# Two VectorE steps change places in the third up-projection unit

## The chip, the cores and the metric

The kernel runs on one core of one Trainium2 chip. Its time is device microseconds of one execution. The kernel before has a median of 1523.43 us over 3 runs (1523.28 to 1523.55). Five engines work side by side and meet through semaphores: TensorE (PE in the profile, its weight loads PEld), VectorE (DVE), ScalarE (ACT), GpSimd (POOL) and SyncE (SP), which issues the DMAs.

## The reference, cut to what matters

One layer of a streaming encoder, in float32, for 1024 tokens of width 1024: a mixer sub-layer (gated linear recurrence beside a spatial gating unit), then a channel sub-layer, then a final norm. The change lies in the channel sub-layer:

```python
h = _modulated_norm(x, norm_ffn_g[l], shift2, scale2)
hid = _causal_dwconv(h @ w_up[l], ffn_conv_w[l], ffn_conv_b[l])   # w_up: 1024 x 6144, conv of width 3
act, val = jnp.split(hid, 2, axis=-1)
x = x + gate2[:, None, :] * ((jax.nn.gelu(act) * val) @ w_down[l])
```

## The kernel before

Everything is transposed: channels on partitions, tokens along the free axis. The up-projection is cut into 24 units `("U", u)`, u from 0 to 23; each makes 128 channels of `act` and the 128 channels of `val` that belong to them, for all 1024 tokens. The third unit, u = 2 (`PLAIN = 2` in the code), is the first that is computed by seven products instead of eight (Strassen-Winograd on a 2 x 2 partition of weights and tokens).

**Two pieces of every number.** A float32 operand is split into a high piece, a copy in a shorter format made by ScalarE (`hi`, L1313), and a low piece, the rest, made by VectorE (`lo`, L1901: `wop low = raw - wop high`). A product of TensorE (`product7`, L886) is 12 matmuls: four k-steps, and for each high x high, high x low, low x high. It waits for the low of its weights, `ready(n)`. The seven weight operands of a unit have the numbers n0 to n0 + 6; the text calls the lows of unit 2 low 1 to low 7 (`lo(n0)` to `lo(n0 + 6)`), and `lo(n0 + 7)`, `lo(n0 + 8)` the next unit's low 1 and 2. Four buffers `wop` hold the pieces and six buffers `raw` the weights themselves.

**The right sides.** Four quarters of the normed activations (`hq`) and four sums or differences of them (`v1q` to `v4q`) lie ready as two pieces each. The lows of the four differences are made once, by `t_low(0)` to `t_low(3)` (L2658, 128 x 2048). The last of them, for `v4q`, is made inside unit 2, whose seventh product is the first to need it.

**Joins.** Products accumulate in PSUM onto each other. ScalarE takes three snapshots of half-made sums (`snap`, L1328), and VectorE adds them where they belong (`join(pos, 0)` to `join(pos, 2)`, L1915; joins 1 to 3 in the text). The seventh product waits for join 2.

**Other steps of VectorE in a unit.** It finishes the unit before: two convolution taps on each of two tiles (`conv_tap`, L2588, reading PSUM) and the product of the gelu and the other half (`gate_mul`, L2600), which waits for the last tap and for the gelu of ScalarE. From every two units it makes parts for the down-projection: `part_sum` (L2625) and `part_low` (L2637), which SyncE stores (`hid_keep`).

**GpSimd** makes the four weight sums of the next unit, four passes of 128 x 512 from SBUF to SBUF (`weight_sums`, L727, L730, L734, L738; passes 1 to 4 in the text). Pass 1 writes into the buffer of the operand of low 6, so it waits for low 6; pass 2 follows pass 1; passes 3 and 4 wait for the next unit's lows 1 and 2.

Each engine runs its instructions in the order in which the program is written. For VectorE this is the loop `for w in range(7)` at L2712: the steps of one unit by slots w, with `lo(n0 + w + 3)` at the end of a slot. The lines that the change touches:

```python
if w >= 4 and not (soon and w < 6):        # L2713
    join(pos, w - 4)
...
if w == 2 and u == PLAIN:                  # L2728
    t_low(3)
...
if n0 + w + 3 < n_ops and (w or kind == "U" and u != PLAIN) and not (late and w == 4)\
        and not (soon and w == 4):
    lo(n0 + w + 3)                         # L2767
```

Of the kernel before, what the change touches and what calls it, by code (L numbers as in the profile page):

```python
# [17 lines left out]
def build(nc, a, out):  # L18
# [7 lines left out]


    _, S, D = a["x"].shape
    KT = D // P
    NB = S // P  # L30
# [42 lines left out]
    with ExitStack() as ctx:  # L73
# [243 lines left out]
        PLAIN = 2  # L317
# [452 lines left out]
        def _(pe):  # L770
# [20 lines left out]
            def param_columns(t):  # L791
                n = sum(n for _, n in ROWS[t])
                return nc.tensor.transpose(ps[0][:, min(t, 1), t * P:t * P + n], prow[0:n, t, :], ident[0:n, 0:n])
# [1092 lines left out]
        def _(dve):  # L1886
# [11 lines left out]
            def lo(n):  # L1898
                dve.wait_ge(f_hi, n + 1)
                kd = depth[n]  # L1900
                V.tensor_tensor(wop[n % 4][:, 1, 0:kd, :], raw[slot_of[n][0]][:, 0:kd, :], wop[n % 4][:, 0, 0:kd, :].bitcast(F32),  # L1901
                                ALU.subtract).then_inc(f_lo, 1)

            def join(pos, i):
                act_t, val_t = BANKS[pos % 2]
                n0, base = first_op[SEQ[pos]], 3 * block_unit[SEQ[pos]]
                u2 = snap_u2r if pos <= AT["ZV", 0] else snap_u2
                p1, p5 = (snap_o1, snap_o5) if SEQ[pos][0] == "O" else (snap_p1, snap_p5)
                out_b, in_b, kept, left, taken = (
                    (act_t[:, 1, :], act_t[:, 1, :], u2, n0 + 3, 3),  # L1910
                    (val_t[:, 1, :], val_t[:, 0, :], p5, n0 + 4, 2),
                    (act_t[:, 0, :], act_t[:, 0, :], p1, n0 + 5, 1))[i]
                dve.wait_ge(*used_at[left])
                dve.wait_ge(snapped, base + taken)
                V.tensor_tensor(out_b, in_b, kept[:, :], ALU.add).then_inc(joined, 1)  # L1915
# [291 lines left out]
            for pos in range(2, AT["B", 0]):  # L2207
                item = SEQ[pos]
                n0 = first_op[item]
# [113 lines left out]
            for pos in range(AT["B", 0], AT["B", 3]):  # L2323
                kind, i = SEQ[pos]
                n0 = first_op[kind, i]
# [162 lines left out]
            for i in range(3):  # L2488
                pos = AT["O", i]
                n0 = first_op["O", i]  # L2490
# [90 lines left out]
            def conv_tap(u, s, d, pos):  # L2581
                dst, src = hidw[hid_slot(u)][:, 1 - s, :], flat(BANKS[pos % 2][s])
                f, k = u + s * FT, FW - 1 - d
                if d == 1:
                    dve.wait_ge(tap0ab, 2 * u + s + 1)
                else:
                    dve.wait_ge(vch, conv_at[u, s])
                tap = V.scalar_tensor_tensor(dst[:, d:S], src[:, 0:S - d],  # L2588
                                             C("ffn_conv_w01" if k < 2 else "ffn_conv_w2", k % 2 * 2 * FT + f), dst[:, d:S],
                                             ALU.mult, ALU.add)  # L2590
                if d == 1:
                    conv_at[u, s] = step_number(tap)
                else:
                    tap.then_inc(taps_done, 1)

            def gate_mul(u):
                w = hidw[hid_slot(u)]
                dve.wait_ge(ga_ready, u + 1)
                dve.wait_ge(taps_done, 2 * u + 2)
                V.tensor_tensor(w[:, 1, :], w[:, 1, :], w[:, 0, :], ALU.mult).then_inc(g_ready, 1)  # L2600
# [47 lines left out]
            def middle_evict(m, pos):  # L2648
                dve.wait_ge(tile_done, m + 1)
                V.scalar_tensor_tensor(xT[:, m, :], flat(BANKS[pos % 2][m % 2]), mod[:, 5 * KT + m:5 * KT + m + 1],  # L2650
                                       xT[:, m, :], ALU.mult, ALU.add).then_inc(down_used, 1)

            def t_low(i):
                dst, src = ((v1q, v1w), (v2q, v2w), (v3q, v3w), (v4q, n21))[i]
                dve.wait_ge(sum_hi, IN_HI + O_PARTS + i + 1)
                if i == 1:
                    dve.wait_ge(t_made, O_SUMS + 4 * KH)
                V.tensor_tensor(dst[:, 1, :, :], src[:, :, :], dst[:, 0, :, :].bitcast(F32), ALU.subtract).then_inc(sum_lo, 1)  # L2658
# [29 lines left out]
            for pos in range(NF + PLAIN, len(SEQ) - 1):  # L2688
                kind, u = SEQ[pos]
                n0 = first_op[kind, u]  # L2690
                j = u // 2 - 1
                if kind == "M":
                    conv_tap(FT - 1, 0, 1, pos - 1)
                    conv_tap(FT - 1, 0, 2, pos - 1)
                    middle_evict(0, pos)
                    lo(n0 + 3)
                    conv_tap(FT - 1, 1, 1, pos - 1)
                    middle_evict(1, pos)
                    conv_tap(FT - 1, 1, 2, pos - 1)
                    middle_evict(2, pos)  # L2700
                    gate_mul(FT - 1)
                    middle_evict(3, pos)
                    lo(n0 + 4)
                    hid_low(FT - 1)
                    middle_evict(4, pos)
                    lo(n0 + 5)
                    for m in range(5, KT):
                        middle_evict(m, pos)
                    lo(n0 + 6)
                    continue  # L2710
                for w in range(7):
                    soon = kind == "U" and u == PLAIN + 2  # L2712
                    if w >= 4 and not (soon and w < 6):  # L2713
                        join(pos, w - 4)
                    if soon and w == 4:
                        join(pos, 0)
                        lo(n0 + w + 3)
                        join(pos, 1)
                    if w == 0:
                        if kind == "D" or u == PLAIN:  # L2720
                            lo(n0 + 3)
                        if kind == "D" and u:
                            evict(pos - 1, 1)
                    if kind == "U":
                        if w == 0:
                            conv_tap(u - 1, 0, 1, pos - 1)
                            conv_tap(u - 1, 0, 2, pos - 1)
                        if w == 2 and u == PLAIN:  # L2728
                            t_low(3)
                        if w in (1, 2):  # L2730
                            conv_tap(u - 1, 1, w, pos - 1)
                        if w == 3:
                            gate_mul(u - 1)
                        if u >= 2 * NP + 1 and w == 6:
                            hid_low(u - 1)
                        if u % 2 and u <= 2 * NP + 1:
                            if u == PLAIN + 1 and w == 0:
                                part_sum(j, "t3")
                            if u == PLAIN + 1 and w == 1:
                                part_low(j, "t3")  # L2740
                            if w == (2 if u == PLAIN + 1 else 0):
                                part_low(j, "b21")
                            if w == 2:
                                part_sum(j, "t4")
                                part_low(j, "t2")
                            if w == (5 if u in LATE else 4):
                                part_low(j, "t4")
                            if w == 5 and u < 2 * NP or w == 6 and u > 2 * NP:
                                part_low(j, "b22")
                            if w == 6 and u < 2 * NP:  # L2750
                                part_low(j + 1, "b11")
                        elif u % 2 == 0 and u <= 2 * NP:
                            if w == 1:
                                part_sum(j, "t1")
                            if w == (5 if u == PLAIN else 4):
                                part_sum(j, "t2")
                                part_low(j, "t1")
                            if w == 5 and u > PLAIN:
                                part_sum(j, "t3")
                            if w == 6 and u > PLAIN:  # L2760
                                part_low(j, "t3")
                    late = kind == "U" and u in LATE
                    if late and w == 5:
                        lo(n0 + 7)
                    if n0 + w + 3 < n_ops and (w or kind == "U" and u != PLAIN) and not (late and w == 4)\
                            and not (soon and w == 4):
                        lo(n0 + w + 3)  # L2767
                    if w == 6 and kind == "D":
                        evict(pos, 0)
# [54 lines left out]
```

## Time and profile before

| | |
|---|---|
| median of 3 runs | 1523.43 us |
| the profiled execution's own time | 1523.99 us |
| its span, first to last instruction | 1522.2 us |
| PE busy | 1500.3 us, 99% of the span |
| DVE busy | 1249.3 us, 82% |
| ACT busy | 821.6 us, 54% |
| POOL busy | 410.7 us, 27% |

All times below are microseconds from the start of the span. Unit 2 lies at about 850 to 872, the last up-projection unit ends at 1272. A row of the timeline has a start, a duration, the engine, the line of the program, the operation with the tiles written and read, and in brackets the idle time of the engine just before it with what ended it. A busy PE is matmuls in a pipeline: one product lasts 2.88 to 3.01 in the rows, and the next begins before its end. VectorE's rows overlap by some 0.08 as well.

### The profile page before, as it was taken

To read this page: it belongs to the slowest core of one execution; us is meant where nothing else is said; L and a number is where in the kernel's file an instruction comes from. 1 tells how busy PE (TensorE), PEld (TensorE's weight loads), DVE (VectorE), ACT (ScalarE), POOL (GpSimd) and SP (SyncE) were. 2 spreads that over 40 slices of the span, in tenths; PEclk is the share of its full clock that TensorE was granted. 3 is DMA by queue.
4 is the path that set the end of the run, shared out by engine and by line. 5 is a ranking of instruction groups with operands and counts; after the bars stand their busy time and mean duration, and the time that the engine had idled before them with its cause. 6 is when DMAs were issued, how large, how long until landed. Compare 5 with 4: busy or idle time off the path is not lost.

```text
span 1522.2 us, 19720 instructions
## 1 busy us (share of the span) xinstructions
PE 1500.3 (99%) x6772; PEld 1233.7 (81%) x6772; DVE 1249.3 (82%) x1577; ACT 821.6 (54%) x1222; POOL 410.7 (27%) x307
## 2 busy tenths in 40 slices
PE   7999999999999999999999999999999999999998
PEld 4788888878888888888887788888888888888887
DVE  6997888777777786688859999999999987777775
ACT  5378988734544473422535555555555553444447
POOL 0024334522223223000100433333333321333324
PEclk9999999999999999999999999999999999999999
DMA  9531233374443364473421244444444436777722
GB/s 348 185 105 55 77 91 92 112 251 138 153 144 123 108 214 145 156 241 102 167 62 42 62 149 164 155 156 152 153 152 152 153 112 231 250 249 249 249 66 112
DMA packets 212227, 231.12 MB, mean 152 GB/s; under 512 B 9920, under 2 KB 164896, under 8 KB 211360
## 3 DMA queue, kind: packets, MB, share of 16 engines
q1 hardware_dynamic: 212128, 229.86, 45.7%
q8 instruction: 55, 0.90, 0.3%
q14 instruction: 44, 0.36, 0.1%
HBM read 167.95 MB, written 61.87 MB: 151 GB/s over the span
## 4 chain that ended last, share of the span: by engine, by line
PE 91%; DVE 6%; issue 1%; DMA 1%; ACT 1%; SPq 0%; DVEq 0%; ACTq 0%
PE ps L886 74%; PE ps L964 4%; PE ps L985 2%; PE ps L1154 1%; PE ps L1250 1%; PE ps L1097 1%; PE ps L1232 1%; PE ps L1014 1%; DVE wop L1901 1%; PE ps L1058 1%; DVE hidw L2588 1%; DMA xtok<-in_x 1%; DVE hq L2531 1%; DVE n L2523 0%; PE ps L1051 0%
## 5 line engine op out<-in xcount | busy, mean ns | idle before, releaser
L1313 ACT ACTIVATE wop<-raw 128x512 fp32r<-128x512 f32 (+1 forms) x541 | 307.1, 571 | 363.2 <-PE ps L886 235.0
L1901 DVE TENSOR_TENSOR wop<-raw,wop 128x512 fp32r<-128x512 f32 (+1 forms) x541 | 372.5, 692 | 120.8 <-ACT wop L1313 119.5
L727 POOL TENSOR_TENSOR raw<-raw,raw 128x512 f32<-128x512 f32 (+1 forms) x69 | 99.4, 1440 | 879.6 <-DVE wop L1901 427.7
L886 PE MATMUL ps<-hq,wop 128*128 128x512 f32 x888 | 214.2, 391 | 1.3 <-DVE wop L1901 0.9
L886 PEld LDWEIGHTS ps<-hq,wop 128*128 128x128 f32 x888 | 166.1, 188 | 38.3 <-DVE hq L2531 1.6
L886 PE MATMUL ps<-dq,wop 128*128 128x512 f32 x840 | 190.6, 389 | 0.0
L886 PE MATMUL ps<-yq,wop 128*128 128x512 f32 x792 | 190.4, 389 | 0.0
L886 PEld LDWEIGHTS ps<-dq,wop 128*128 128x128 f32 x840 | 157.7, 188 | 32.7
L886 PEld LDWEIGHTS ps<-yq,wop 128*128 128x128 f32 x792 | 148.5, 188 | 31.1 <-DVE wop L1901 0.2
L1915 DVE TENSOR_TENSOR ps<-ps,snap_p 128x512 f32<-128x512 f32 x136 | 94.5, 695 | 53.4 <-PE ps L886 52.8
L1328 ACT ACTIVATE snap_p<-ps 128x512 f32<-128x512 f32 x136 | 81.2, 597 | 101.7 <-PE ps L886 101.5
L2588 DVE SCALAR_TENSOR_TENSOR hidw<-ps,pc,hidw 128x1023 f32<-128x1023 f32 x96 | 122.4, 1276 | 0.9
L734 POOL TENSOR_TENSOR raw<-raw,raw 128x512 f32<-128x512 f32 (+1 forms) x69 | 91.6, 1328 | 93.7 <-DVE wop L1901 92.7
L738 POOL TENSOR_TENSOR raw<-raw,raw 128x512 f32<-128x512 f32 (+1 forms) x69 | 82.7, 1199 | 92.2 <-DVE wop L1901 91.2
L730 POOL TENSOR_TENSOR raw<-raw,raw 128x512 f32<-128x512 f32 (+1 forms) x69 | 93.9, 1361 | 9.9
L1731 ACT ACTIVATE hidw<-ps,pc 128x1024 f32<-128x1024 f32 x48 | 57.5, 1207 | 15.3 <-PE ps L886 12.2
L964 PE MATMUL ps<-yb_split,wop 128*128 128x512 f32 x288 | 65.7, 389 | 0.0
L886 PE MATMUL ps<-t2q,wop 128*128 128x512 f32 x264 | 65.1, 395 | 0.0
L886 PE MATMUL ps<-v4q,wop 128*128 128x512 f32 x264 | 63.5, 389 | 1.0 <-DVE ps L1915 1.0
L886 PE MATMUL ps<-t1q,wop 128*128 128x512 f32 x264 | 64.3, 392 | 0.0
L886 PE MATMUL ps<-t3q,wop 128*128 128x512 f32 x264 | 64.2, 392 | 0.0
L1328 ACT ACTIVATE snap_u<-ps 128x512 f32<-128x512 f32 x62 | 37.0, 597 | 50.2 <-PE ps L886 50.1
(288 smaller groups left out, 2584.7 us busy)
## 6 DMA issues: line engine op xcount, KB each, us to landing
dq<-hid_keep SPq DMA_DIRECT2D x35, 1024.0 KB, 7.1
raw<-in_w_in SPq DMA_DIRECT2D x96, 256.0 KB, 4.2
raw<-in_w_up SPq DMA_DIRECT2D x96, 256.0 KB, 3.3
hid_keep<-part_b SPq DMA_DIRECT2D x40, 512.0 KB, 3.0
hid_keep<-part_t SPq DMA_DIRECT2D x20, 512.0 KB, 3.1
raw<-in_w_down SPq DMA_DIRECT2D x80, 128.0 KB, 2.3
ada_w<-in_w_ada SPq DMA_DIRECT2D x8, 1024.0 KB, 11.4
gate_keep<-tg SPq DMA_DIRECT2D x16, 512.0 KB, 4.7
```

The costliest lines, as they stand in the source:

```text
L727: nc.gpsimd.tensor_tensor(s1, a21, a22, ALU.add).then_inc(s_made, 1)
L730: nc.gpsimd.tensor_tensor(a21, a11, a21, ALU.subtract).then_inc(s_made, 1)
L734: nc.gpsimd.tensor_tensor(a11, s1, a11, ALU.subtract).then_inc(s_made, 1)
L738: nc.gpsimd.tensor_tensor(s1, a12, a11, ALU.subtract).then_inc(s_made, 1)
L886: done = nc.tensor.matmul(bank, left[:, w, lk, :], right[:, x, rk, :], start=(first and w == 0 and x == 0), stop=(last and w == 1), skip_g ...
L964: done = nc.tensor.matmul(psum[:, h, :], wop[n % 4][:, w, k % KH, :], right(k, x, h), start=(k == 0 and w == 0 and x == 0), stop=(k == KT ...
L1313: nc.scalar.activation(wop[n % 4][:, 0, 0:depth[n], :], raw[slot][:, 0:depth[n], :], ACT.Copy).then_inc(f_hi, 1)
L1328: nc.scalar.activation(dst[:, :], src, ACT.Copy).then_inc(snapped, 1)
L1731: nc.scalar.activation(hidw[slot][:, 1 - s, :], flat(BANKS[pos % 2][s]), ACT.Identity, bias=C("ffn_conv_b", f), scale=C("ffn_conv_w2", f)) ...
L1901: V.tensor_tensor(wop[n % 4][:, 1, 0:kd, :], raw[slot_of[n][0]][:, 0:kd, :], wop[n % 4][:, 0, 0:kd, :].bitcast(F32), ALU.subtract).then_in ...
L1915: V.tensor_tensor(out_b, in_b, kept[:, :], ALU.add).then_inc(joined, 1)
L2588: tap = V.scalar_tensor_tensor(dst[:, d:S], src[:, 0:S - d], C("ffn_conv_w01" if k < 2 else "ffn_conv_w2", k % 2 * 2 * FT + f), dst[:, d:S ...
```

## The change

Both edits are in VectorE's order in unit 2, the slots w = 2 to w = 5. Low 6 moves from behind the tap to ahead of `t_low(3)`, past `t_low(3)` and one tap. Join 2 moves ahead of the next unit's low 1. Nothing else is added, dropped or moved, and no buffer changes.

```diff
-                    if w >= 4 and not (soon and w < 6):
+                    if w >= 4 and not (soon and w < 6) and not (kind == "U" and u == PLAIN and w == 5):
                         join(pos, w - 4)
...
                         if w == 2 and u == PLAIN:
+                            lo(n0 + 5)
                             t_low(3)
+                        if w == 4 and u == PLAIN:
+                            join(pos, 1)
...
                     if n0 + w + 3 < n_ops and (w or kind == "U" and u != PLAIN) and not (late and w == 4)\
-                            and not (soon and w == 4):
+                            and not (soon and w == 4) and not (kind == "U" and u == PLAIN and w == 2):
                         lo(n0 + w + 3)
```

The order on VectorE in unit 2, before, from low 5 (`wop3_73<-raw4_68`) to the next unit's low 2 (`wop3_73<-raw2_66`):

```order
L1901 TENSOR_TENSOR wop3_73<-raw4_68,wop3_73 128x512 [waits f_hi]
L2658 TENSOR_TENSOR v4q_60<-n21_202,v4q_60 128x2048 [waits sum_hi]
L2588 SCALAR_TENSOR_TENSOR hidw1_165<-ps3,pc_210,hidw1_165 128x1022 [waits vector_step]
L1901 TENSOR_TENSOR wop0_70<-raw2_66,wop0_70 128x512 [waits f_hi]
L2600 TENSOR_TENSOR hidw1_165<-hidw1_165 128x1024 [waits taps_done,ga_ready]
L1901 TENSOR_TENSOR wop1_71<-raw0_64,wop1_71 128x512 [waits f_hi]
L1915 TENSOR_TENSOR ps2<-ps2,snap_u2_76 128x512 [waits snapped,used]
L1901 TENSOR_TENSOR wop2_72<-raw1_65,wop2_72 128x512 [waits f_hi]
L1915 TENSOR_TENSOR ps1<-ps1,snap_p5_75 128x512 [waits snapped,used]
L2625 TENSOR_TENSOR raw_t1_177<-hidw1_165,raw_t0_176 128x512 [waits part_raw,g_ready]
L2637 TENSOR_TENSOR part_b0_168<-raw_t0_176,part_b0_168 128x512 [waits part_raw,part_hi]
L1901 TENSOR_TENSOR wop3_73<-raw2_66,wop3_73 128x512 [waits f_hi]
```

The same place with what the change takes away and puts in:

```order
 L1901 TENSOR_TENSOR wop3_73<-raw4_68,wop3_73 128x512
+L1901 TENSOR_TENSOR wop0_70<-raw2_66,wop0_70 128x512
 L2658 TENSOR_TENSOR v4q_60<-n21_202,v4q_60 128x2048
 L2588 SCALAR_TENSOR_TENSOR hidw1_165<-ps3,pc_210,hidw1_165 128x1022
-L1901 TENSOR_TENSOR wop0_70<-raw2_66,wop0_70 128x512
 L2600 TENSOR_TENSOR hidw1_165<-hidw1_165 128x1024
 L1901 TENSOR_TENSOR wop1_71<-raw0_64,wop1_71 128x512
 L1915 TENSOR_TENSOR ps2<-ps2,snap_u2_76 128x512
+L1915 TENSOR_TENSOR ps1<-ps1,snap_p5_75 128x512
 L1901 TENSOR_TENSOR wop2_72<-raw1_65,wop2_72 128x512
-L1915 TENSOR_TENSOR ps1<-ps1,snap_p5_75 128x512
 L2625 TENSOR_TENSOR raw_t1_177<-hidw1_165,raw_t0_176 128x512
```

Low 6 (`wop0_70<-raw2_66`) now stands between low 5 and the difference's low, and the last tap (L2588) stands directly ahead of `gate_mul` (L2600), which waits for it by `taps_done`. Join 2 (`ps1<-ps1,snap_p5_75`) follows join 1 directly. The orders of PE, ACT, POOL and SP are the same as before.

## Rows read from the trace of the kernel before

**Rows 1.** The page: busy time of each engine

```profile
PE 1500.3 (99%) x6772; PEld 1233.7 (81%) x6772; DVE 1249.3 (82%) x1577; ACT 821.6 (54%) x1222; POOL 410.7 (27%) x307
```

**Rows 2.** Timeline of PE, products 4 to 7: start, duration

```profile
858.57 2.88 PE L886 MATMUL ps<-hq,wop 128*128 128x512 f32 x12
861.29 2.94 PE L886 MATMUL ps<-v3q,wop 128*128 128x512 f32 x12
865.13 3.01 PE L886 MATMUL ps<-hq,wop 128*128 128x512 f32 x12 [0.91 <-DVE wop L1901]
869.19 3.01 PE L886 MATMUL ps<-v4q,wop 128*128 128x512 f32 x12 [1.04 <-DVE ps L1915]
```

**Rows 3.** Timeline of DVE, from the difference's low to a part_low

```profile
861.00 2.29 DVE L2658 TENSOR_TENSOR v4q<-n,v4q 128x2048 fp32r<-128x2048 f32 x1
863.20 1.28 DVE L2588 SCALAR_TENSOR_TENSOR hidw<-ps,pc,hidw 128x1022 f32<-128x1022 f32 x1
864.40 0.68 DVE L1901 TENSOR_TENSOR wop<-raw,wop 128x512 fp32r<-128x512 f32 x1
865.00 1.22 DVE L2600 TENSOR_TENSOR hidw<-hidw 128x1024 f32<-128x1024 f32 x1
866.13 0.69 DVE L1901 TENSOR_TENSOR wop<-raw,wop 128x512 fp32r<-128x512 f32 x1
866.73 0.69 DVE L1915 TENSOR_TENSOR ps<-ps,snap_u 128x512 f32<-128x512 f32 x1
867.33 1.19 DVE L1901 TENSOR_TENSOR wop<-raw,wop 128x512 fp32r<-128x512 f32 x1
868.45 0.69 DVE L1915 TENSOR_TENSOR ps<-ps,snap_p 128x512 f32<-128x512 f32 x1
869.05 1.15 DVE L2625 TENSOR_TENSOR raw_t<-hidw,raw_t 128x512 f32<-128x512 f32 x1
870.31 1.59 DVE L2637 TENSOR_TENSOR part_b<-raw_t,part_b 128x512 fp32r<-128x512 f32 x1
```

**Rows 4.** Timeline: high 6 on ACT; a high and the low that waits for it

```profile
861.22 0.62 ACT L1313 ACTIVATE wop<-raw 128x512 fp32r<-128x512 f32 x1
...
892.70 0.63 ACT L1313 ACTIVATE wop<-raw 128x512 fp32r<-128x512 f32 x1 [2.29 <-POOL raw L734]
...
893.36 1.55 DVE L1901 TENSOR_TENSOR wop<-raw,wop 128x512 fp32r<-128x512 f32 x1 [0.15 <-ACT wop L1313]
```

**Rows 5.** Timeline: passes of POOL, and two DVE rows beside them

```profile
848.32 2.21 POOL L734 TENSOR_TENSOR raw<-raw,raw 128x512 f32<-128x512 f32 x1 [6.27 <-DVE wop L1901]
851.16 3.27 POOL L738 TENSOR_TENSOR raw<-raw,raw 128x512 f32<-128x512 f32 x1 [0.63 <-DVE wop L1901]
865.16 2.82 POOL L727 TENSOR_TENSOR raw<-raw,raw 128x512 f32<-128x512 f32 x1 [10.72 <-DVE wop L1901]
868.12 1.53 POOL L730 TENSOR_TENSOR raw<-raw,raw 128x512 f32<-128x512 f32 x1
872.58 1.29 POOL L738 TENSOR_TENSOR raw<-raw,raw 128x512 f32<-128x512 f32 x1 [1.23 <-DVE wop L1901]
...
849.30 1.79 DVE L1901 TENSOR_TENSOR wop<-raw,wop 128x512 fp32r<-128x512 f32 x1
853.21 1.77 DVE L2637 TENSOR_TENSOR part_b<-hidw,part_b 128x512 fp32r<-128x512 f32 x1
```

**Rows 6.** Timeline of DVE and PEld where the fifth unit begins

```profile
889.40 0.90 DVE L2637 TENSOR_TENSOR part_t<-hidw,part_t 128x512 fp32r<-128x512 f32 x1 [0.80 <-ACT part_t L1769]
890.23 1.28 DVE L1901 TENSOR_TENSOR wop<-raw,wop 128x512 fp32r<-128x512 f32 x2
...
891.02 2.60 PEld L886 LDWEIGHTS ps<-hq,wop 128*128 128x128 f32 x12 [0.20 <-issue]
```

**Rows 7.** Stretches: length, PE, PEld, DVE, ACT, POOL busy, granted clock, DMA share, GB/s

```profile
861.00:872.00 11.00, 9.05 (x39) 6.74 (x38) 10.90 (x12) 3.12 (x6) 5.91 (x3) 1.00 0.08 24
...
33.50:36.90 3.40, 3.40 (x7) 1.69 (x6) 3.40 (x4) 1.51 (x2) 0.00 (x0) 0.50 1.06 369
```

## The prediction

> **What bounds the kernel now.** I read the page first: TensorE's matmuls are busy 99% of the span [rows 1], so time can be won only where it stands still, and any new pause of it is lost. Next TensorE's timeline around the third unit (U2). Products follow each other by 2.72 us from start to start there (858.57, 861.29), and twice this breaks [rows 2]: product 6 starts at 865.13 after 0.91 us, put down to a weights' low of VectorE, and product 7 at 869.19 after 1.04 us, put down to a join. Product 6 could have started about 861.29 + 2.72 = 864.01, product 7 some 2.8 us after product 6. Then VectorE's timeline of the same stretch [rows 3]: it has not one pause there, each row beginning about 0.08 us before the one ahead of it ends. So VectorE's row of work is what TensorE waits for; what counts is where in this row low 6 and join 2 end. Last, for the two things that can get in its way, ScalarE's high 6 [rows 4] and GpSimd's passes over the next unit's weights [rows 5].
>
> **The change, part by part.** No instruction is added or dropped, and PE, ACT, POOL and SP keep their orders; the sums below are start times on VectorE, made against the profiled execution (span 1522.2, its own time 1523.99; that is 0.56 above the 1523.43 median of the runs shown, so I add the difference found here to the median).
>
> *Low 6 goes ahead of the fourth difference's low.* Low 5 leaves the place free at 861.00, where the difference's low starts now. But low 6 needs high 6, and ScalarE makes it only from 861.22 to 861.84; it comes behind other work that the change does not touch. Where VectorE really waits for a high, its low starts 0.03 us after the high's end (893.36 after 892.70 + 0.63) [rows 4]. So low 6 runs from 861.87 to 862.55, and everything behind it on VectorE is late by 0.87. For product 6 that is ample: it starts at about 864.05 instead of 865.13, and its 0.91 us pause goes. Nothing else can start on that: TensorE's next product needs join 2.
>
> *Low 6 leaves the place between the second tap and gate_mul.* The difference's low then runs from 862.47 to 864.76 (2.29), the tap from 864.67 to 865.95 (1.28). gate_mul waits for that very tap. Until now low 6 stood between them and covered this. A VectorE instruction that waits for the one right ahead of it starts 0.10 us after its end (part_low at 870.31 after 869.05 + 1.15) [rows 3]; so gate_mul starts at 866.05 and not at 865.87: another 0.18.
>
> *Join 2 ahead of the next unit's low 1.* Join 2 no longer stands behind a row that takes 868.45 - 867.33 = 1.12 [rows 3]; 0.51 of it is no work (1.19 against 0.68 of the same form). The next low 1 comes 0.6 later than join 2; product 1 of the next unit needs it some 2.8 us after product 7 starts, so that costs nothing.
>
> Without GpSimd, join 2 would start at 868.45 + 0.87 + 0.18 - 1.12 = 868.38, and product 7 0.07 earlier than now. So the two moves nearly cancel, and GpSimd decides.
>
> *GpSimd's passes.* Pass 1 for the next unit waits for low 6 (it reuses its buffer) and started 0.08 us behind it, at 865.16 [rows 5]. It now starts at 862.63, in the difference's low. Passes and VectorE's subtractions out of two SBUF buffers do not run side by side: the pass of 851.16 ended at 854.43 and held a part_low that needs 0.68 to 854.98; the one of 848.32 ended at 850.53 and held a low from 849.30 to 851.09 [rows 5]. The held row ends 0.55 after the pass; a pass that has waited ends some 1.16 after the row that kept it out (867.98 against 866.82) [rows 3, 5]. Instructions that read PSUM (taps, joins) are not held: join 1 takes its 0.69 inside a pass. So pass 1 waits for the difference's low, runs beside the tap and ends at 864.76 + 1.16 = 865.92, free of cost (it cost 0.51 in the next low 1). Pass 2 starts 0.14 after it (868.12 after 867.98 [rows 5]), at 866.06: the same instant as gate_mul, to 0.01. Until now it ran beside join 2 and cost 0.47 in the part_sum behind it (1.15 against 0.68). Now two instructions with two SBUF operands stand there, gate_mul and low 7, and only then join 1.
>
> If gate_mul gets in first (866.05 to 867.27), pass 2 has the next turn: to 868.43, and low 7 ends at 868.98 in place of 867.87, 1.11 later. Join 1 follows at 868.89, join 2 at 869.49 to 870.18, product 7 at 870.23. If the pass gets in first, it takes its 1.29 (as at 872.58 [rows 5]) to 867.35, and gate_mul, 0.13 of which lies inside it as with the held rows (0.68 - 0.55), ends 1.22 - 0.13 later at 868.44, join 2 at 870.24: nearly the same price. So join 2 moves by 0.87 + 0.18 - 1.12 + 1.11 = +1.04, and so does product 7; its pause grows from 1.04 to about 3.3 us, since product 6 was early. The price of this unseen meeting lies between 0 (the pass runs fully beside the joins; it can't pay anything back, since its old cost is already taken off) and 1.17 (the pass first); I take 1.11, because the held rows of [rows 5] show such a whole price.
>
> In the Trainium skill, "SBUF — State Buffer", section "Who interferes with whom", the shared port pair goes to whichever of the two issues first for its whole instruction and the other blocks fully. By that rule low 7 is held in any case, and the sum is +1.04 at product 7 with no other end. The rows agree at 848.32 and 851.16, but not at 865.16: there gate_mul was under way, the pass was waiting, and low 7 (866.13, 0.69) still went ahead of it unheld [rows 3, 5]. The measurement decides; the rule is too strict here.
>
> *What becomes of it.* VectorE's row up to the next low 2 sums to 0.87 + 0.18 + 1.11 - 0.51 - 0.47 = +1.18; passes 3 and 4 hold as much as before. In the next unit TensorE has no pause, but its last reserve is thin: the first low of the fifth unit comes at 890.23 behind a part_low that waited 0.80 for ScalarE at 889.40, a chain that begins on VectorE, and TensorE's load for that product starts at 891.02, only 0.1 behind the low's end (890.23 + 0.68) [rows 3, 6]. These shift with VectorE, so the final loss is VectorE's, 1.18, not 1.04. With TensorE busy 99% of the span [rows 1], no later pause is there to give it back. The store queue holds the next loads behind the part that now comes later; that is part of the same shift. Forecast: 1523.43 + 1.2 = 1524.6 us.
>
> **The rivals.** *The pass is passed over* (no change at all). Low 7 goes ahead of pass 2 as it did of pass 1 at 865.16 [rows 5]; there are two such cases, the other alike and two units later. Then pass 2 runs beside joins 1 and 2, join 2 starts at 868.38, and VectorE's row is at 0.87 + 0.18 - 0.51 - 0.47 = +0.07. TensorE gains 0.06 and loses it again to that row: 1523.5. For it: these two; against it: the two of 848.32 and 851.16, where the pass had its turn, and that gate_mul must first win a dead heat. A little over half of a half: 0.27.
>
> *The clock falls in the longer pause* (slower). This is the other side. TensorE stands still for 3.3 us in one piece, three times its longest pause in the rows here; the granted clock is 1.00 from 861 to 872 [rows 7]. The one drop inside this trace, 33.5 to 36.9, stood at 0.50, that is 1.2 in place of 2.4 GHz, for 3.4 us [rows 7]. At half speed a stretch of that length costs at most 1.7: 1523.43 + 1.18 + 1.7 = 1526.3; part of it may fall into the pause itself, so 1525.0 to 1526.3. About 0.2%, 3.05 us, is what a measurement of this kernel can tell from no change; from (3.05 - 1.18) x 2 = 3.7 us at half clock on, this case would be beyond it. For it: the pause; against it: both pauses of now left the clock at 1.00. 0.22. The Trainium skill says in "TensorE: Matmul & The Clock Gate", Part 1, that the half rate is the default and activity releases it; no row here shows a pause of this size.
>
> *The two pauses go as the words of the change suggest* (faster). This needs high 6 by 861.00 and pass 2 out of the way: -0.87 more than the second case, 1522.6. ScalarE's row speaks against it: 0.04.
>
> **How the numbers follow.** Forecast 0.45, passed over 0.27, clock 0.22, faster 0.04, unseen 0.02. The forecast's own range is 1524.3 to 1524.9. The range reaches from the second case less the spread of the runs (1523.2) to the clock case but for its end (1526.0). All cases lie within 3.05 us of now but the far end of the clock case. Same 0.95, slower 0.04, faster 0.01.
>
> **What would show it.** Low 6 at about 861.9 with some 0.8 idle, released by ScalarE. Product 6 at 864.0 without a pause. Pass 1 at 862.6, about 3.3 long. gate_mul at 866.05 or held by pass 2; low 7 or gate_mul with about 1.1 too much; join 2 at about 869.5 and product 7 at 870.2. The fifth unit's first product 1.2 later than now. A low 7 of 0.69 directly behind gate_mul would make the second case right, a granted clock under 1 at 866 to 877 the third. Low 6 without an idle would overturn the first step.

## The result and the profile after

The changed kernel takes 1525.50 us (median of 22 runs, 1524.80 to 1527.09); the kernel before 1523.61 (22 runs, 1523.14 to 1524.19). The ratio is 1.0013, with an interval of 1.0007 to 1.0019. So the change costs 1.89 us, a small loss that this interval tells from no change and that lies within the 0.2% which the prediction took for no change. The time is inside the stated range (1523.2 to 1526.0), but 0.9 above the 1524.6 forecast and outside the forecast's own 1524.3 to 1524.9.

The profiled execution of after has a time of its own of 1525.26 and a span of 1523.5. Executions differ by some tenths of a us before they reach the third unit (product 4 starts at 858.57 before [rows 2] and at 857.93 after, with nothing changed ahead of it). So I count from product 4's start in each trace. First TensorE's timeline of after, products 4 to 7, the next unit's first product, and the fifth unit's first and sixth; it answers to [rows 2].

```profile
857.93 2.89 PE L886 MATMUL ps<-hq,wop 128*128 128x512 f32 x12
860.66 2.92 PE L886 MATMUL ps<-v3q,wop 128*128 128x512 f32 x12
863.42 2.88 PE L886 MATMUL ps<-hq,wop 128*128 128x512 f32 x12
869.57 4.36 PE L886 MATMUL ps<-v4q,wop 128*128 128x512 f32 x12 [3.27 <-DVE ps L1915]
873.76 2.90 PE L886 MATMUL ps<-hq,wop 128*128 128x512 f32 x12
...
892.82 2.88 PE L886 MATMUL ps<-hq,wop 128*128 128x512 f32 x12
...
906.42 2.88 PE L886 MATMUL ps<-hq,wop 128*128 128x512 f32 x12
```

The fourth, fifth and sixth products now follow each other by 2.73 and 2.76: the pause before product 6 is gone. In place of two pauses of 0.91 and 1.04 stands one of 3.27, before product 7, and product 7 itself takes 4.36 where it took 3.01. The next unit's first product and the fifth unit's first six in the kernel before, and the weight loads (PEld) of the fifth unit's third and fourth:

```profile
872.04 2.88 PE L886 MATMUL ps<-hq,wop 128*128 128x512 f32 x12
...
891.08 2.97 PE L886 MATMUL ps<-hq,wop 128*128 128x512 f32 x12
893.88 2.88 PE L886 MATMUL ps<-v1q,wop 128*128 128x512 f32 x12
896.60 3.00 PE L886 MATMUL ps<-v2q,wop 128*128 128x512 f32 x12
899.57 3.01 PE L886 MATMUL ps<-hq,wop 128*128 128x512 f32 x12
902.42 2.88 PE L886 MATMUL ps<-v3q,wop 128*128 128x512 f32 x12
905.14 2.88 PE L886 MATMUL ps<-hq,wop 128*128 128x512 f32 x12
...
896.58 2.60 PEld L886 LDWEIGHTS ps<-v2q,wop 128*128 128x128 f32 x12 [0.24 <-ACT snap_p L1328]
899.57 2.59 PEld L886 LDWEIGHTS ps<-hq,wop 128*128 128x128 f32 x12 [0.40 <-ACT snap_p L1328]
```

Three of these five steps from start to start, 891.08 to 905.14, are long: 2.80, 2.97 and 2.85 against the plain 2.72 are 0.46 lost to small waits. No matmul row bears an idle note for them, but the weight loads do: 0.20 at the first product [rows 6], then 0.24 and 0.40 for snapshots of ScalarE. After has none of it: 892.82 to 906.42 is five times 2.72. With these two lists the loss is a sum. Product 7 stands 11.64 behind product 4 (10.62 before): +1.02. The step from product 7 to the next product is 4.19 (2.85): +1.34. From there to the fifth unit's first product nothing changes (19.06 against 19.04): +0.02. The fifth unit takes 13.60 to its sixth product in place of 14.06: -0.46. Together +1.92, beside the measured 1.89.

Then VectorE's timeline, which answers to [rows 3], with ScalarE's high 6 [rows 4] and GpSimd's passes 1 and 2 [rows 5] behind it.

```profile
861.22 0.69 DVE L1901 TENSOR_TENSOR wop<-raw,wop 128x512 fp32r<-128x512 f32 x1 [0.78 <-ACT wop L1313]
861.83 2.28 DVE L2658 TENSOR_TENSOR v4q<-n,v4q 128x2048 fp32r<-128x2048 f32 x1
864.04 1.27 DVE L2588 SCALAR_TENSOR_TENSOR hidw<-ps,pc,hidw 128x1022 f32<-128x1022 f32 x1
865.41 1.22 DVE L2600 TENSOR_TENSOR hidw<-hidw 128x1024 f32<-128x1024 f32 x1
866.55 1.75 DVE L1901 TENSOR_TENSOR wop<-raw,wop 128x512 fp32r<-128x512 f32 x1
868.23 0.68 DVE L1915 TENSOR_TENSOR ps<-ps,snap_u 128x512 f32<-128x512 f32 x1
868.83 0.68 DVE L1915 TENSOR_TENSOR ps<-ps,snap_p 128x512 f32<-128x512 f32 x1
869.43 0.67 DVE L1901 TENSOR_TENSOR wop<-raw,wop 128x512 fp32r<-128x512 f32 x1
870.03 0.68 DVE L2625 TENSOR_TENSOR raw_t<-hidw,raw_t 128x512 f32<-128x512 f32 x1
870.81 1.58 DVE L2637 TENSOR_TENSOR part_b<-raw_t,part_b 128x512 fp32r<-128x512 f32 x1
...
860.57 0.62 ACT L1313 ACTIVATE wop<-raw 128x512 fp32r<-128x512 f32 x1
...
862.00 3.28 POOL L727 TENSOR_TENSOR raw<-raw,raw 128x512 f32<-128x512 f32 x1 [8.21 <-DVE wop L1901]
865.42 2.34 POOL L730 TENSOR_TENSOR raw<-raw,raw 128x512 f32<-128x512 f32 x1
```

Low 6 stands idle for 0.78 until high 6 is made. gate_mul starts 0.10 after its tap ends. Pass 2 starts 0.01 behind gate_mul, waits for it, and holds low 7, which takes 1.75 in place of 0.69. The next low 1 (869.43) and the part_sum (870.03) are back at 0.67 and 0.68 (1.19 and 1.15 before). The part_low behind them starts 12.88 after product 4 (11.74 in the kernel before [rows 2, 3]): VectorE is 1.14 late, where the forecast summed to 1.18. Last the stretches of after, in the columns of [rows 7]:

```profile
866.00:869.04 3.04, 0.30 (x2) 0.00 (x0) 3.04 (x4) 0.00 (x0) 1.76 (x1) 1.00 0.00 0
869.04:872.45 3.41, 2.88 (x7) 2.31 (x8) 3.31 (x5) 0.57 (x1) 1.66 (x1) 0.50 0.00 0
```

The granted clock is 1.00 through the pause but for its last half us, then 0.50, that is 1.2 GHz, for 3.41 us; before, it is 1.00 in the whole stretch [rows 7]. The first 2.88 us of product 7 ran in that half-clock piece. So VectorE's row came as forecast, and the case of the falling clock came on top of it.

### The profile page after: what moved, and what is told of

The parts are those of the page before. It is cut to its first block, busy times and chain, and to the rows that moved or that the text cites. A ratio compares the mean times of both kernels' runs of the same rounds, so it can differ in the third digit from the quotient of the medians.

```text
span 1523.5 us, 19720 instructions
## 1 busy us (share of the span) xinstructions
PE 1500.3 (98%) x6772; PEld 1234.9 (81%) x6772; DVE 1251.0 (82%) x1577; ACT 821.8 (54%) x1222; POOL 411.9 (27%) x307
## 4 chain that ended last, share of the span: by engine, by line
PE 91%; DVE 6%; issue 1%; ACT 1%; DMA 1%; SPq 0%; DVEq 0%; ACTq 0%
PE ps L886 73%; PE ps L964 4%; PE ps L985 2%; PE ps L1154 1%; PE ps L1250 1%; PE ps L1097 1%; PE ps L1232 1%; PE ps L1014 1%; DVE wop L1901 1%; PE ps L1058 1%; DMA xtok<-in_x 1%; DVE hidw L2588 1%; DVE hq L2531 1%; DVE n L2523 0%; PE ps L1051 0%
## 5 line engine op out<-in xcount | busy, mean ns | idle before, releaser
L2588 DVE SCALAR_TENSOR_TENSOR hidw<-ps,pc,hidw 128x1023 f32<-128x1023 f32 x96 | 122.5, 1277 | 0.9
```

What stands on the lines that cost most here:

```text
L2588: tap = V.scalar_tensor_tensor(dst[:, d:S], src[:, 0:S - d], C("ffn_conv_w01" if k < 2 else "ffn_conv_w2", k % 2 * 2 * FT + f), dst[:, d:S ...
```

## The experiments

All are edits of the changed kernel; none leaves work out. The table gives the start of products counted from product 4's in the profiled execution ("P7" is product 7, "5P6" the fifth unit's sixth product), whether the clock went to 0.50 at the pause there, and the median of the runs against the kernel before in the same session.

| kernel | P6 | P7 | next P1 | 5P1 | 5P6 | 0.50 there | time, before | ratio (interval) |
|---|---|---|---|---|---|---|---|---|
| before | 6.56 | 10.62 | 13.47 | 32.51 | 46.57 | no | | |
| after | 5.49 | 11.64 | 15.83 | 34.89 | 48.49 | yes | 1525.50, 1523.61 | 1.0013 (1.0007 to 1.0019) |
| e1 | 5.48 | 12.25 | 16.71 | 35.78 | 49.38 | yes | 1526.60, 1523.87 | 1.0018 (1.0009 to 1.0027) |
| e2 | 6.57 | 9.52 | 12.37 | 32.63 | 46.73 | no | 1523.72, 1523.87 | 1.0000 (0.9991 to 1.0008) |
| e3 | 5.48 | 10.58 | 13.47 | 32.76 | 46.88 | no | 1524.79, 1523.87 | 1.0006 (0.9997 to 1.0015) |
| e3 again | 5.52 | 10.58 | 14.86 | 34.10 | 47.70 | yes | 1524.78, one run | |
| e4 | 7.44 | 11.70 | 14.56 | 33.65 | 47.79 | no | 1524.73, 1523.87 | 1.0007 (0.9998 to 1.0016) |
| e5 | 5.50 | 10.81 | 13.66 | 32.75 | 46.87 | no | 1523.99, 1523.79 | 1.0003 (0.9994 to 1.0012) |
| e6 | 5.50 | 9.26 | 12.12 | 32.40 | 46.51 | no | 1523.22, 1523.79 | 0.9996 (0.9987 to 1.0005) |
| e7 | 5.53 | 8.40 | 11.25 | 31.44 | 45.54 | no | 1522.50, 1523.79 | 0.9992 (0.9983 to 1.0001) |

**e1: the low's move alone.**

```
-  if w >= 4 and not (soon and w < 6) and not (kind == "U" and u == PLAIN and w == 5):
+  if w >= 4 and not (soon and w < 6):
...
-  if w == 4 and u == PLAIN:
-      join(pos, 1)
```

> Low 6 ahead of the difference's low as in the change, join 2 left behind the next unit's low 1. My theory (VectorE's row sets the loss: 0.87 for high 6, 0.18 uncovered ahead of gate_mul, 1.11 for pass 2 in front of low 7, 0.51 saved in the next low 1): product 7 of unit 2 starts 1.65 later than before, counted from product 4 (12.27 in place of 10.62), its pause is 3.9 long, and VectorE's row is 1.18 late at the next low 2. Time 1524.8 to 1526.0, the upper end with a clock drop. Rival, that the join's new place does the harm: as before, 1523.6.

TensorE's timeline of e1, product 7 and the product behind it (product 4 starts at 857.96):

```profile
870.21 4.61 PE L886 MATMUL ps<-v4q,wop 128*128 128x512 f32 x12 [3.89 <-DVE ps L1915]
874.67 2.92 PE L886 MATMUL ps<-hq,wop 128*128 128x512 f32 x12
```

A stretch inside product 7, in the columns of [rows 7]:

```profile
872.00:874.00 2.00, 2.00 (x6) 1.51 (x6) 2.00 (x4) 0.51 (x1) 1.07 (x1) 0.50 0.43 155
```

Product 7's place came as expected, 12.25 against 12.27, behind a pause of 3.89, and it takes 4.61, with the clock at 0.50. VectorE is 0.94 late at the next low 2, a little less than the 1.18 expected. The time is 0.6 above the expected range: I had laid the clock's cost on VectorE's row, but what is late here is TensorE. Its own sum holds: +1.63 at product 7, +1.61 in the step behind it (4.46 against 2.85), and -0.43 in what follows, +2.81 beside the measured 2.73. So this half of the change is the loss.

**e2: the join's move alone.**

```
-                            lo(n0 + 5)
...
-  and not (soon and w == 4) and not (kind == "U" and u == PLAIN and w == 2):
+  and not (soon and w == 4):
```

> Join 2 ahead of the next unit's low 1 as in the change, low 6 left where it was. My theory: join 2 starts 1.12 earlier, product 7 1.05 earlier than before (9.57 after product 4 in place of 10.62), but VectorE's row is as long as before (0 to +0.1 at the next low 2), and the fifth unit's first product waits for its low, so the gain is given back there: the fifth unit's sixth product 46.5 to 46.7 after product 4 (before 46.57), time 1523.5 to 1523.8. Rival, that TensorE's pause at product 7 sets the loss by itself: 1.05 is kept, time 1522.6.

TensorE's timeline of e2, product 7 and the fourth unit's third product (product 4 starts at 858.32):

```profile
867.84 3.02 PE L886 MATMUL ps<-v4q,wop 128*128 128x512 f32 x12
...
876.89 3.02 PE L886 MATMUL ps<-v2q,wop 128*128 128x512 f32 x12 [0.60 <-ACT snap_p L1328]
```

Join 2 behind join 1 takes the pause before product 7 away: product 7 comes 1.10 earlier. 0.76 of that is lost at the fourth unit's third product, which waits for a snapshot of ScalarE (it starts 3.48 after the product of 873.41, in place of 2.72), and the rest by the fifth unit's first product (32.63 against 32.51). I had expected the loss at the fifth unit alone; the end, no gain, is as expected. Here TensorE did not keep a lead that VectorE and ScalarE did not have.

**e3: pass 2 of the next unit held back until low 7 is done.**

```
   # weight_sums, ahead of pass 2
+  if item == ("U", PLAIN + 1):
+      pool.wait_ge(f_lo, n0)
```

> The whole change, and GpSimd's pass 2 for the fourth unit waits for low 7 as well. My theory: pass 1 still runs beside the tap, low 7 takes 0.69, pass 2 runs beside joins 1 and 2, product 7 starts 10.55 after product 4 (before 10.62, the change 11.64), the pause is 2.2, the clock stays at 1.00, VectorE is 0.1 to 0.2 late at the next low 2; time 1523.7 to 1523.9. Rival, that the wait for high 6 is the loss and the pass only moves: product 7 at 11.5 and time 1524.8 or more.

Its timeline: VectorE's gate_mul and low 7, GpSimd's pass 2, and TensorE's product 7 (line numbers are two higher in this kernel):

```profile
865.98 1.23 DVE L2602 TENSOR_TENSOR hidw<-hidw 128x1024 f32<-128x1024 f32 x1
867.12 0.69 DVE L1903 TENSOR_TENSOR wop<-raw,wop 128x512 fp32r<-128x512 f32 x1
...
867.98 1.26 POOL L732 TENSOR_TENSOR raw<-raw,raw 128x512 f32<-128x512 f32 x1 [2.14 <-DVE wop L1903]
...
869.07 3.06 PE L888 MATMUL ps<-v4q,wop 128*128 128x512 f32 x12 [2.22 <-DVE ps L1917]
```

With the pass behind it, low 7 takes 0.69 and not 1.75: product 7 gains 1.06 on after and stands 0.04 ahead of its old place. The 1.1 in low 7 is thus pass 2's. The time does not follow: 1524.79, some 1.0 above what I expected, although this profiled execution, with a time of its own of 1524.15, shows no half clock there. So the same kernel was run once more.

> The kernel with pass 2 behind low 7, a second look, since its other runs lie 0.3 to 0.7 above the profiled one. If the clock does it: the granted clock is at 0.50 for some 3.4 us from about 867 to 870 on, product 7 lasts longer, the fifth unit's sixth product is at 47.4 to 47.6 after product 4 (first look 46.88), time 1524.7 to 1524.9. If this execution has no drop: 46.9 and 1524.1. If something else does it: no drop, and still 1524.8.

TensorE's product 7 in this execution:

```profile
868.82 4.48 PE L888 MATMUL ps<-v4q,wop 128*128 128x512 f32 x12 [2.19 <-DVE ps L1917]
```

Product 7 and its pause stand at the same place, but it takes 4.48. The stretch behind its start, in the columns of [rows 7]:

```profile
870.04:873.45 3.41, 3.41 (x9) 2.65 (x9) 3.31 (x5) 1.00 (x2) 2.18 (x2) 0.50 0.21 77
```

Same kernel, same pause of 2.2, with the clock down here and not in the other execution. So this pair shows the price, with one execution on each side: the next product is 1.39 later and the fifth unit's sixth 0.82. The times differ by 0.63 (1524.78 against 1524.15), mostly since the second execution had reached product 4 already 0.25 earlier. Eight of the 11 timed runs of e3 lie at 1524.32 to 1524.86 with a mean clock of 0.997, as this one has; three at 1524.02 to 1524.36 have 0.999, as the profile without the drop. That the drop makes up the slower eight is the likely reading; none of the eight was traced.

**e4: the same row of VectorE, the pause cut in two.** Product 6 is made to wait for the second tap, though it needs nothing of it; no row of VectorE shown here waits for product 6.

```
   # unit(), ahead of product 6
+  if item == ("U", PLAIN):
+      pe.wait_ge(taps_done, 2 * PLAIN)
```

> The whole change, and TensorE's product 6 of unit 2 waits for the unit before's last tap too, so the one long pause becomes two. My theory: product 6 at 7.4 after product 4, product 7 unchanged at 11.64, pauses of about 1.9 and 1.3, the clock stays at 1.00, and what is left is VectorE's lateness: the fifth unit's sixth product 47.7 after product 4 (before 46.57, the change 48.49), time 1524.8. Rival, that the clock drop costs nothing in the end because later waits absorb it: 1525.5 as with the change. Second rival, that the drop comes in spite of the split: 1.2 GHz is seen again near 870.

The timeline of e4: TensorE's products 6 and 7, VectorE's gate_mul and low 7, and pass 2 (lines of the VectorE helpers are two higher):

```profile
865.63 3.01 PE L886 MATMUL ps<-hq,wop 128*128 128x512 f32 x12 [1.80 <-DVE hidw L2590]
869.89 3.02 PE L886 MATMUL ps<-v4q,wop 128*128 128x512 f32 x12 [1.25 <-DVE ps L1917]
...
865.68 2.35 DVE L2602 TENSOR_TENSOR hidw<-hidw 128x1024 f32<-128x1024 f32 x1
867.95 0.68 DVE L1903 TENSOR_TENSOR wop<-raw,wop 128x512 fp32r<-128x512 f32 x1
...
865.65 1.29 POOL L730 TENSOR_TENSOR raw<-raw,raw 128x512 f32<-128x512 f32 x1
```

The stretch about both pauses, in the columns of [rows 7]:

```profile
862.00:874.00 12.00, 8.95 (x39) 6.76 (x38) 11.79 (x13) 1.80 (x4) 6.80 (x4) 1.00 0.10 31
```

TensorE now waits on purpose, stands still for nearly as long in sum (1.80 + 1.25 against 3.27), and the kernel is faster than after: by 0.77 in the medians (1524.73 against 1525.50), by 1.03 where each is set against the kernel before of its own session (+0.86 and +1.89), by 0.70 at the fifth unit's sixth product (47.79 against 48.49). The medians come from two sessions, and the intervals of the two ratios overlap, so the positions carry more than the times. The clock stays at 1.00 in the profiled execution; three of the 11 runs have a mean clock of 0.997 (1524.63 to 1525.08), and whether it fell at the pause in them is not shown. Expected were 47.7 and 1524.8. This is the direct test of the two terms: VectorE's row alone costs 1.22 at that product, near the forecast's 1.18, and the long pause with its half-clock piece the other 0.70. Here pass 2 won the dead heat: gate_mul takes 2.35 and low 7 0.68, the other branch of the forecast, at nearly the same price, as it had said.

**e5: high 6 made earlier.** ScalarE makes highs 5 and 6 ahead of the work that stood before them.

```
   t_high(3); snap(pos, 1)
+  hi(n0 + 4)
+  hi(n0 + 5)
...
-  if n0 + w + 3 < n_ops:
+  if n0 + w + 3 < n_ops and not (kind == "U" and u == PLAIN and w in (1, 2)):
```

> The whole change, and ScalarE makes highs 5 and 6 ahead of the gelu, in its idle time, so low 6 need not wait. My theory: the 0.87 is gone and nothing else: low 6 at 2.43 after product 4 without an idle, product 6 at 5.5, pass 2 still in the way of gate_mul or low 7, product 7 at 10.8 (the change 11.63, before 10.62), VectorE 0.3 late at the next low 2 (13.6, before 13.25). Without a clock drop the fifth unit's sixth product at 46.9 and time 1524.2; with the drop behind the 2.4 long pause 1524.9. Rival, that the pass is passed over: product 7 at 9.7. Rival, that the 0.87 is hidden anyway: product 7 stays at 11.6.

The timeline of e5: VectorE's lows 5 and 6 in one row, its low 7, and TensorE's product 7:

```profile
859.85 1.28 DVE L1903 TENSOR_TENSOR wop<-raw,wop 128x512 fp32r<-128x512 f32 x2
...
865.78 1.77 DVE L1903 TENSOR_TENSOR wop<-raw,wop 128x512 fp32r<-128x512 f32 x1
...
868.81 3.01 PE L886 MATMUL ps<-v4q,wop 128*128 128x512 f32 x12 [2.43 <-DVE ps L1917]
```

Lows 5 and 6 now stand back to back, without the idle, and low 7 is held all the same. Product 7 comes 0.83 earlier than in after, the sixth of the fifth unit at 46.87, as expected (10.8 and 46.9). The wait for high 6, 0.87 in the forecast, is thus worth 0.83 at product 7. The time is 1523.99, 0.2 under what I expected without a drop of the clock; its four runs at 1524.47 to 1524.69 have a mean clock of 0.997, the other seven 0.999.

**e6: gate_mul behind both joins.**

```
   join(pos, 1)
+  gate_mul(u - 1)
...
-  if w == 3:
+  if w == 3 and u != PLAIN:
```

> The whole change, and gate_mul of unit 2 moved behind join 2, so low 7 covers the tap's end and both joins come before gate_mul; low 6 still waits for its high. My theory: pass 2 runs beside the joins, product 7 at 9.25 after product 4 (before 10.62), pause 0.9, no clock drop; VectorE's row about as long as before (next low 2 at 13.15, before 13.25), and so the fifth unit's sixth product at 46.4 to 46.6 (before 46.57): time 1523.7 to 1523.9, the gain of TensorE in unit 2 given back at the fifth unit. Rival, that the gain of 1.4 at product 7 is kept: 1522.4.

The timeline of e6: TensorE's product 7 and the fourth unit's third product, and pass 2:

```profile
867.23 3.02 PE L886 MATMUL ps<-v4q,wop 128*128 128x512 f32 x12 [0.88 <-DVE ps L1915]
...
876.33 3.06 PE L886 MATMUL ps<-v2q,wop 128*128 128x512 f32 x12 [0.64 <-ACT snap_p L1328]
...
865.48 1.63 POOL L730 TENSOR_TENSOR raw<-raw,raw 128x512 f32<-128x512 f32 x1
```

Now low 7 and the joins stand behind the tap, and pass 2 runs beside the joins (1.63 long). The pause falls from 3.27 to 0.88 and product 7 stands at 9.26, as expected (9.25). The next pause, for the snapshot, gives most of it back. The time is 0.5 below what I expected, of which the positions (46.51 against 46.57) show 0.06. In the profiled execution the rest lies ahead of product 4, which starts 0.60 earlier than before (857.97 against 858.57) with nothing changed there; why the median of 11 runs is low too is open, and the interval takes in no change.

**e7: e5 and e6 together.**

> Highs 5 and 6 ahead of the gelu and gate_mul behind join 2, on top of the whole change. My theory: product 6 at 5.5, product 7 at 8.3 without a pause (before 10.62), VectorE's next low 2 at 12.3 (0.98 earlier than before), and this 0.98 is what is left at the fifth unit: its sixth product at 45.6 (before 46.57), time 1522.8 to 1523.0, about 1 below before. Rival, that TensorE's 2.3 at product 7 is kept: 1521.5. Rival, that passes 3 and 4 take VectorE's saving: as before, 1523.8.

The timeline of e7: the same two products, VectorE's low 7 and, behind the joins, its gate_mul, and pass 2:

```profile
866.25 3.02 PE L886 MATMUL ps<-v4q,wop 128*128 128x512 f32 x12
...
875.35 3.02 PE L886 MATMUL ps<-v2q,wop 128*128 128x512 f32 x12 [0.65 <-ACT snap_p L1328]
...
864.30 0.68 DVE L1903 TENSOR_TENSOR wop<-raw,wop 128x512 fp32r<-128x512 f32 x1
...
866.10 1.22 DVE L2602 TENSOR_TENSOR hidw<-hidw 128x1024 f32<-128x1024 f32 x1
...
864.49 1.65 POOL L730 TENSOR_TENSOR raw<-raw,raw 128x512 f32<-128x512 f32 x1
```

Both pauses ahead of products 6 and 7 are gone (the one for the snapshot stays, 0.65), no VectorE row ahead of product 7 is held, and product 7 comes 2.22 earlier than before; 1.03 of it is left at the fifth unit's sixth product. The time is 1522.50 (1522.11 to 1523.06), 0.3 below the expected 1522.8 to 1523.0 and 1.3 under before, of which the positions show 1.03. The interval of the ratio reaches 1.0001, but the slowest of its 11 runs is under the quickest of the 27 of before (1523.08). It is the quickest version here, 3.0 under the change's median of another session. By its trace the idea behind the two moves works once high 6 is there in time and gate_mul does not stand where pass 2 arrives.

## Why the prediction was right, and where it was wrong

1525.50 lies in the stated range because that range reached up to the falling clock, a case with a chance of 0.22; the forecast's own case gave too little. Its sum for VectorE came out; what it had TensorE make of that did not.

- *Low 6 waits for high 6: right.* Idle 0.78 for ScalarE was shown where some 0.8 was forecast; e5 takes the wait away and gets the 0.83 back at product 7.
- *gate_mul without cover: right.* It starts 0.10 behind its tap (865.41 after 864.04 + 1.27) and no longer 0.08 ahead of the end of a row between them. (The row behind the forecast's 0.10 gives 0.11: 870.31 after 870.20.)
- *Join 2 without the next low 1 ahead of it: right.* e2 alone moves product 7 by 1.10; the forecast took 1.12.
- *Pass 2 and low 7: right.* Low 7 is 1.06 too long, forecast 1.11, and e3 shows that the pass does it. The case of the pass that is passed over (0.27) did not come. What the Trainium skill says in "SBUF — State Buffer", section "Who interferes with whom", that the first to issue has the shared ports for its whole instruction and the other blocks fully, agrees with after (gate_mul at 865.41 keeps out the pass of 865.42, and this holds low 7 to 1.75) and with e4 (the pass first, gate_mul held to 2.35). Low 7 of before, which passed the waiting pass [rows 3, 5], stays against it; why it went otherwise there is not settled. That low 7 is held in any case, as the prediction read the rule, was too much: in e4 gate_mul was held and low 7 took 0.68, for nearly the same sum.
- *Product 7: right.* +1.02 against +1.04, pause 3.27 against about 3.3.
- *"With TensorE busy 99% of the span, no later pause is there to give it back": wrong.* The 0.46 of small waits in the fifth unit gives back what TensorE is late beyond VectorE. On the matmuls these waits show only as steps of 2.80, 2.97 and 2.85 from start to start. The first is the thin reserve that the forecast saw at [rows 6], read from the wrong side; the weight loads put the others down to ScalarE's snapshots. VectorE's lateness was not given back here (1.22 in e4), TensorE's beyond it was in part (1.39 became 0.82 in the two executions of e3).
- *The clock stays, and the final loss is VectorE's 1.18: this step failed.* The falling clock had a chance of 0.22. Against it stood that both pauses of before left the clock at 1.00; that tells nothing of one three times as long. In the profiled execution the clock was at 0.50 for 3.41 us [rows 7 had 3.4], and the fifth unit's first product came 2.38 later than before, not 1.2. So this rival's mechanism was right, and 1525.50 lies in its 1525.0 to 1526.3. Its price of at most 1.7 over VectorE's row was 1.34 in the step behind product 7, and 0.6 to 1.0 at the end (0.70 to 1.03 by e4, 0.63 and 0.82 by the two executions of e3), because of the waits of the point above. Of the 1.92 at the fifth unit's sixth product the forecast's 1.18 leaves 0.74 for it.

What stays open: in which runs the clock falls. The mean clock doesn't sort them, since a second half-clock piece near 33.5 us is in some executions (before, after, e3 again, e4) and not in others (e1, e2, e3, e5, e6, e7), and after's runs at 0.999 (1524.80 to 1525.94) are no quicker than those at 0.997 (1525.15 to 1525.70). After's three slowest runs, 1526.68 to 1527.09, have 0.996, less than any traced execution; no trace shows where their clock fell. That the price of the drop is part of the 1.89 rests on the profiled executions of after and e4 and on the two of e3.

## What to carry to other kernels

Before an instruction is moved to the head of a row, look at what releases it: here 0.87 of the waiting was only moved from TensorE to VectorE, where everything behind it is late. When work shifts by a us, read off anew which instruction stands beside each pass of GpSimd: beside pass 2 the joins, which read PSUM, took their usual 0.69 (e6), while a subtraction out of two SBUF buffers paid 1.06 (low 7 of after). Be wary of adding up two pauses into one: in this kernel the same VectorE row cost 0.7 to 1.0 less with TensorE's 3 us split into 1.80 and 1.25.

## What the runs showed of the hardware

The granted clock fell to 0.50 in one execution of e3 after a pause of 2.19 and not in another after one of 2.22; it fell after 3.27 (after) and 3.89 (e1), and not in the profiles with 2.43 (e5), 1.80 and 1.25 (e4). The piece at 0.50 lasted 3.41 in after and in e3's second execution; it began 0.53 ahead of product 7's start in the one, 1.22 behind it in the other.

Of a GpSimd pass and a VectorE instruction with two SBUF operands that meet within some hundredths of a us either may be first: pass 2 was 0.01 behind gate_mul in after and 0.03 ahead of it in e4. The sum is nearly the same, but it falls on another instruction: low 7 takes 1.75 in the one, gate_mul 2.35 in the other.
